# First pair of a seven-product down projection: another product order, other places for its weight sums, and two small moves on VectorE

## The chip, the cores and the metric

The kernel runs on one core of a Trainium2 chip. Its time is the device time of one execution in microseconds (us), taken as the median of several runs. Five engines work beside each other, each in the order of its own program: PE (TensorE) multiplies, DVE (VectorE) and ACT (ScalarE) work elementwise, POOL (GpSimd) works elementwise too, and SP (SyncE) issues the loads from HBM. Semaphores are the only link between them.

## What is computed

The reference is two transformer-like blocks on 512 tokens (528 in the first block, with 16 meta tokens), width 1024. Each block has two feed-forward layers (FFNs) around a mixer; the four FFNs are the same computation with different weights:

```python
def swiglu(x, w_in, w_out):
    gu = x @ w_in
    return (jax.nn.silu(gu[..., :D_FF]) * gu[..., D_FF:]) @ w_out
...
h = h + 0.5 * rmsnorm(swiglu(rmsnorm(h, gn[0]), ffn_w_in[i, 0], ffn_w_out[i, 0]), gn[1])
```

`D_FF` is 2816. The change lies in the last product, `@ w_out`, 2816 by 1024, of each of the four FFNs (numbered 0 to 3 here). Everything is float32.

## The kernel before

**Splitting.** PE multiplies in a reduced float32 format, so each operand is split into a high part (a copy, mostly on ACT: `hi`) and a low part (operand minus high part, on DVE or POOL: `lo`), and a product is three matmuls: high by high, high by low, low by high. Weight blocks of 128x1024 lie in four slots each of `raw` (as loaded), `whi`, `wlo`, and `stage` (sums of blocks).

**The down projection.** Of the 22 row tiles of `w_out`, 6 are multiplied directly, one unit per output tile (8 units; ACT's `keep(j)` moves unit j's result to SBUF). The other 16 are multiplied pair by pair (`PAIRS` is 4; a pair is two output tiles of 128 columns) by a scheme of seven products M1 to M7 in place of eight. A pair's weights are four loaded blocks A11, A21, A12, A22 and four sums: S1 = A21 + A22, S2 = S1 - A11, S3 = A11 - A21, S4 = A12 - S2 (functions `s1` to `s4`, DVE). The hidden values have blocks B and sums T in the same way (`x_hi`, `x_lo`, `x_sum`), and they are made once, during the units and the first pair. Products use M1: A11, M2: A12, M3: S4, M4: A22, M5: S1, M6: S2, M7: S3; each is 8 row tiles by 3 matmuls, 24 matmuls of 256 columns (264 in FFN 0), line L3396.

**Orders.** Everything is ordered by hand: `PRODUCTS`, `D_HI`, `LO_DVE`, `LO_POOL` and `D_POSTS` must name the order in which PE, ACT, DVE and POOL go, because each entry becomes a semaphore count. DVE also adds each product's bank to the output (`post`, lines L2174 in FFN 0 and 1 and L2176 in FFN 2 and 3): k1 takes M1, u2 takes M6, k5 M5, c22 M7, k23 M3, c21 M4. Products share PSUM banks, so M6 waits for k1, M7 for u2, M3 for k5, and M4 for c22. S1 and S2 of the first three pairs are written to PSUM banks 6 and 7 (`sums`), one after the other, so S2 waits until S1's low part is done. A slot of `whi` and `wlo` is given by a product's place in the order (`nth`), and ACT may write it when the product four places earlier is done. A block of `raw` may be loaded for the next pair when its readers are done (`block_read`); SP issues A11, A21, A12, A22 in that order.

**Lines.** DVE: `s1` L2226, `s2` L2237, `s3` L2241, `s4` L2250 (L2253 in the last pair); `lo` of a sum in PSUM L2262, of a raw block L2266, of a staged sum L2268; `x_lo` L2205; `merge` (FFN 2 and 3 only) L2212; `gained` (FFN 3 only) L2289; low parts of the next stage's input L1863. ACT: `hi` L970, `x_hi` L955, `keep` L947. POOL: `lo` L638. In the first pair POOL makes the low parts of A11 and A12, and then waits for the low part of T4 before it goes on to the second pair's A11.

Of the kernel before, what the change touches and what calls it, by code (L numbers as in the profile page):

```python
# [127 lines left out]
def program(nc, dram, out, stop=99):  # L128
# [210 lines left out]
    DOWN_TAKES = dict(mult=24, w_hi=27, w_sum=16, w_lo_dve=28, w_lo_pool=13, kept=8, x_diff=14, x_hi=14)  # L339
# [601 lines left out]
    def act_down(act, i):  # L941
# [15 lines left out]
        def hi(d, block):  # L957
# [1232 lines left out]
    def dve_down(v, i):  # L2190
# [24 lines left out]
        def s1(d):  # L2215
            down_loaded(v, i, d, "A21")
            down_loaded(v, i, d, "A22")
            if d == 0:
# [37 lines left out]
        def lo(d, block):  # L2256
# [1903 lines left out]
```

## Time and profile before

| | us |
|---|---|
| median of 3 runs | 1949.59 |
| range of the runs | 1948.12 to 1954.43 |
| span of the profiled execution | 1948.1 |
| PE, matmul busy in that span | 1907.9 (98%) |
| DVE busy | 1400.1 (72%) |
| ACT busy | 1027.5 (53%) |
| POOL busy | 878.1 (45%) |

The page lists busy time per engine. A matmul's row lasts longer than the step to the next one (rows of 0.28 us start about 0.12 us apart), so PE reads as busy across a short stall, and its idle figure is smaller than the time lost. Lost time is therefore read here from the starts of matmuls. In a timeline row the columns are start, duration, engine, line, operation, output and inputs, shape, count, and in brackets the idle time before it with what ended it. The span and the median differ by 1.5 us.

### The profile page before, as it was taken

To read this page: it belongs to the slowest core of one execution; us is meant where nothing else is said; L and a number is where in the kernel's file an instruction comes from. 1 tells how busy PE (TensorE), PEld (TensorE's weight loads), DVE (VectorE), ACT (ScalarE), POOL (GpSimd) and SP (SyncE) were. 2 spreads that over 40 slices of the span, in tenths; PEclk is the share of its full clock that TensorE was granted. 3 is DMA by queue.
4 is the path that set the end of the run, shared out by engine and by line. 5 is a ranking of instruction groups with operands and counts; after the bars stand their busy time and mean duration, and the time that the engine had idled before them with its cause. 6 is when DMAs were issued, how large, how long until landed. Compare 5 with 4: busy or idle time off the path is not lost. (4 is left out here: it accounts for less than half of the span.)

```text
span 1948.1 us, 38305 instructions
## 1 busy us (share of the span) xinstructions
PE 1907.9 (98%) x13945; PEld 1751.9 (90%) x13945; DVE 1400.1 (72%) x1936; ACT 1027.5 (53%) x1695; POOL 878.1 (45%) x525
## 2 busy tenths in 40 slices
PE   8999999999999999999999999999999999999998
PEld 8999999997779899989989998897775778999898
DVE  5977687785455877676787768877756548776876
ACT  5566654535324566664466666445346445666543
POOL 3455453643325455553545555344441044555533
PEclk9999999999999999999999999999999999999999
DMA  6233333322412233333423334243311022333332
GB/s 178 66 103 101 97 88 102 105 58 65 111 52 71 82 108 108 105 101 87 120 65 109 108 108 116 80 117 104 81 44 55 2 86 77 108 107 105 101 87 87
DMA packets 344605, 178.05 MB, mean 91 GB/s; under 512 B 18715, under 2 KB 340118, under 8 KB 344494
## 3 DMA queue, kind: packets, MB, share of 16 engines
q1 hardware_dynamic: 342640, 175.46, 31.8%
q8 instruction: 74, 1.21, 0.2%
q10 hardware_dynamic: 1854, 1.07, 0.2%
q14 instruction: 37, 0.30, 0.1%
HBM read 174.42 MB, written 2.10 MB: 91 GB/s over the span
## 5 line engine op out<-in xcount | busy, mean ns | idle before, releaser
L3458 PE MATMUL ps<-xop,whi 128*128 128x256 f32 (+1 forms) x4032 | 722.8, 282 | 8.6 <-DVE sq L2005 5.9
L3458 PEld LDWEIGHTS ps<-xop,whi 128*128 128x128 f32 x4032 | 621.1, 189 | 10.8 <-DVE sq L2005 6.8
L3458 PE MATMUL ps<-xop,wlo 128*128 128x256 f32 (+1 forms) x2016 | 568.1, 282 | 0.0
L536 POOL TENSOR_TENSOR wlo<-raw,whi 128x1024 fp32r<-128x1024 f32 x94 | 233.9, 2497 | 371.0 <-ACT whi L702 360.8
L3458 PEld LDWEIGHTS ps<-xop,wlo 128*128 128x128 f32 x2016 | 379.7, 188 | 0.0
L597 POOL TENSOR_TENSOR wlo<-raw,whi 128x512 fp32r<-128x512 f32 x212 | 278.2, 1323 | 220.7 <-ACT whi L832 219.9
L3396 PE MATMUL ps<-xop,whi 128*128 128x256 f32 (+1 forms) x896 | 215.1, 284 | 6.7 <-DVE hT L2176 1.8
L3129 PE MATMUL ps<-xhi,whi 128*128 128x512 f32 (+2 forms) x624 | 210.8, 367 | 1.7 <-DVE xlo L1863 1.6
L3129 PE MATMUL ps<-xlo,whi 128*128 128x512 f32 (+2 forms) x624 | 204.0, 356 | 0.0
L3129 PE MATMUL ps<-xhi,wlo 128*128 128x512 f32 (+2 forms) x624 | 203.5, 355 | 0.0
L3396 PE MATMUL ps<-hid_r,whi 128*128 128x256 f32 (+1 forms) x768 | 191.3, 283 | 2.9 <-DVE hT L2176 2.4
L638 POOL TENSOR_TENSOR wlo<-raw,whi 128x1024 fp32r<-128x1024 f32 x44 | 114.7, 2614 | 165.9 <-ACT whi L970 111.2
L597 POOL TENSOR_TENSOR wlo<-stage,whi 128x512 fp32r<-128x512 f32 x72 | 94.2, 1309 | 179.8 <-ACT whi L832 179.8
L3396 PEld LDWEIGHTS ps<-xop,whi 128*128 128x128 f32 x896 | 155.4, 188 | 9.8 <-DVE hT L2176 2.2
L832 ACT ACTIVATE whi<-ps 128x512 fp32r<-128x512 f32 x180 | 107.9, 599 | 106.6 <-DVE ps L1974 79.9
L3396 PE MATMUL ps<-xop,wlo 128*128 128x256 f32 (+1 forms) x576 | 162.2, 282 | 0.0
L1994 DVE TENSOR_TENSOR wlo<-ps,whi 128x512 fp32r<-128x512 f32 x180 | 123.4, 685 | 47.9 <-ACT whi L832 47.6
L3396 PEld LDWEIGHTS ps<-hid_r,whi 128*128 128x128 f32 x768 | 135.7, 188 | 5.1 <-DVE hT L2176 4.0
L832 ACT ACTIVATE whi<-raw 128x512 fp32r<-128x512 f32 x216 | 134.2, 621 | 0.0
L3129 PEld LDWEIGHTS ps<-xhi,whi 128*128 128x128 f32 (+1 forms) x624 | 109.5, 187 | 27.0 <-issue 6.0
L702 ACT ACTIVATE whi<-raw 128x1024 fp32r<-128x1024 f32 x96 | 99.8, 1051 | 63.2 <-PE ps L3129 49.0
L3129 PEld LDWEIGHTS ps<-xlo,whi 128*128 128x128 f32 (+1 forms) x624 | 110.0, 187 | 18.3 <-issue 2.2
(469 smaller groups left out, 3950.9 us busy)
## 6 DMA issues: line engine op xcount, KB each, us to landing
raw<-in_ffn_w_in SPq DMA_DIRECT2D x88, 512.0 KB, 3.8
raw<-in_ffn_w_gate SPq DMA_DIRECT2D x44, 512.0 KB, 3.8
raw<-in_ffn_w_up SPq DMA_DIRECT2D x44, 512.0 KB, 3.8
raw<-in_ffn_w_out SPq DMA_DIRECT2D x32, 512.0 KB, 4.2
raw<-in_ffn_w_down SPq DMA_DIRECT2D x32, 512.0 KB, 4.2
raw<-in_a_w_in SPq DMA_DIRECT2D x24, 512.0 KB, 3.9
raw<-in_w_in SPq DMA_DIRECT2D x19, 512.0 KB, 3.9
raw<-in_ffn_w_out SPq DMA_DIRECT2D x16, 384.0 KB, 3.5
```

The lines of the kernel that those rows point to most:

```text
L536: pool.tensor_tensor(wlo[:, u % SLOTS, :], raw[:, u % SLOTS, :], whi[:, u % SLOTS, :].bitcast(F32), ALU.subtract).then_inc(lo_done, 1)
L597: pool.tensor_tensor(operand(wlo, i, name), source, operand(whi, i, name).bitcast(F32), ALU.subtract) \
L638: ins = pool.tensor_tensor(to, source, down_operand(whi, i, d, block).bitcast(F32), ALU.subtract)
L702: act.activation(whi[:, s, :], raw[:, s, :], ACT.Copy).then_inc(hi_done, 1)
L832: ins = act.activation(operand(whi, i, name), source, ACT.Copy)
L1994: v.tensor_tensor(operand(wlo, i, name), sum_place(i, name), operand(whi, i, name).bitcast(F32), ALU.subtract).then_inc(s["w_lo_dve"], 1)
L3129: ins = pe.matmul(o, lhs[l], x[r], start=first and n == 0, stop=last and n == 2)
L3396: ins = pe.matmul(ps[:, bank_, 0:h], weights[l][:, k * P:(k + 1) * P], parts[r][:, k % 4, :], start=start and k == 0 and q == 0, stop=k == ...
L3458: ins = pe.matmul(to, w[l][:, k * P:(k + 1) * P], x[r][:, k * h:(k + 1) * h], start=start and k == 0 and q == 0, stop=k == 3 and q == 2, s ...
```

## The change

In pair 0, PE's order becomes M1, M2, M6, M5, M7, M3, M4 (M2 and M5 change places), and ACT's high parts follow it (A12 first, S1 last of its three). S2 gets PSUM banks of its own, 4 and 5, so it no longer waits for S1's low part. S3 is written over A21 in `raw`, so it needs no free slot of `stage` and is made right behind S2, ahead of k1; in return the next load into that place waits for S3's low part. In FFN 2 and 3, `merge(2)` and `merge(3)` move: one ahead of `s1`, one ahead of the two low parts. Behind k1 on DVE, k5 moves from second place to behind S4's low part, A22's low part moves ahead of B22's second low part, and the low part of pair 1's A11 is added, which POOL made before; POOL's wait for T4 goes. In pairs 1, 2 and 3, u2 moves ahead of a low part, and `gained` behind S4's low part.

```diff
-    DOWN_TAKES = dict(mult=24, w_hi=27, w_sum=16, w_lo_dve=28, w_lo_pool=13, kept=8, x_diff=14, x_hi=14)
+    DOWN_TAKES = dict(mult=24, w_hi=27, w_sum=16, w_lo_dve=29, w_lo_pool=12, kept=8, x_diff=14, x_hi=14)
...
-            sp.wait_ge(*down_sum(i, d, "S3"))
+            sp.wait_ge(*(down_lo(i, d, "S3") if d == 0 else down_sum(i, d, "S3")))
...
         for d in (1, 2):
-            if d == 1:
-                pool.wait_ge(*x_lo_made(i, "T4", 1))
-            lo(d, "A11")
+            if d == 2:
+                lo(d, "A11")
             lo(d, "A12")
...
-        hi(0, "S1")
+        hi(0, "A12")
         keep(6)
         hi(0, "S2")
         keep(7)
-        hi(0, "A12")
+        hi(0, "S1")
...
-    PRODUCTS = [["M1", "M5", "M6", "M2", "M7", "M3", "M4"]] * 3 + [["M1", "M2", "M6", "M4", "M7", "M5", "M3"]]
+    PRODUCTS = [["M1", "M2", "M6", "M5", "M7", "M3", "M4"]] + [["M1", "M5", "M6", "M2", "M7", "M3", "M4"]] * 2 + [["M1", "M2", "M6", "M4", "M7", "M5", "M3"]]
...
+    def sum_bank(d, block):
+        return ps[:, 4:6, :] if (block, d) == ("S2", 0) else ps[:, 6:8, :]
+
+    def s3_place(i, d):
+        return down_raw(i, d, "A21") if d == 0 else down_operand(stage, i, d, "S3")
...
+            elif d == 1:
+                v.wait_ge(*down_sum(i, 0, "S2"))
+                v.wait_ge(*down_lo(i, 0, "S1"))
...
-            if d < PAIRS - 1:
+            if d == 0:
+                v.wait_ge(*x_lo_made(i, "T2", 1))
+                v.wait_ge(*x_sum_made(i, "T4", 1))
+                to = sum_bank(d, "S2")
+            elif d < PAIRS - 1:
...
         def s3(d):
-            down_slot_free(v, i, d, "S3")
-            v.tensor_tensor(down_operand(stage, i, d, "S3"), down_raw(i, d, "A11"), down_raw(i, d, "A21"), ALU.subtract) \
+            if d == 0:
+                v.wait_ge(*down_sum(i, d, "S1"))
+            else:
+                down_slot_free(v, i, d, "S3")
+            v.tensor_tensor(s3_place(i, d), down_raw(i, d, "A11"), down_raw(i, d, "A21"), ALU.subtract) \
...
         merge(1)
+        merge(2)
         s1(0)
+        s2(0)
+        s3(0)
+        merge(3)
+        lo(0, "S2")
         lo(0, "S1")
-        s2(0)
-        lo(0, "S2")
-        merge(2)
-        merge(3)
         a, b, c = down_banks(0)
         post(0, "k1", "M1", 0, 0, a)
-        s3(0)
         x_lo("T3", 0)
-        post(0, "k5", "M5", 1, 1, c)
         x_lo("T3", 1)
         lo(0, "S3")
         s4(0)
+        x_lo("B22", 0)
         post(0, "u2", "M6", 0, 1, a)
-        x_lo("B22", 0)
+        lo(0, "A22")
         x_lo("B22", 1)
         lo(0, "S4")
-        lo(0, "A22")
+        post(0, "k5", "M5", 1, 1, c)
+        x_lo("T4", 0)
         post(0, "c22", "M7", 1, 1, a, "k5")
-        x_lo("T4", 0)
+        lo(1, "A11")
         x_lo("T4", 1)
         s1(1)
...
             s4(d)
+            post(d, "u2", "M6", 0, 1, a)
+            lo(d, "S4")
             gained(d - 1)
-            lo(d, "S4")
-            post(d, "u2", "M6", 0, 1, a)
...
+        post(3, "u2", "M6", 0, 1, a)
         lo(3, "S1")
-        post(3, "u2", "M6", 0, 1, a)
...
+            multiply(d, *(("M2", b) if d == 0 else ("M5", c)), True).then_inc(s["mult"], 1)
+            pe.wait_ge(*down_post(i, d, "k1"))
+            multiply(d, "M6", a, False).then_inc(s["mult"], 1)
             if d == 0:
                 pe.wait_ge(s["kept"], down_at[i]["kept"] + KD)
-            multiply(d, "M5", c, True).then_inc(s["mult"], 1)
-            pe.wait_ge(*down_post(i, d, "k1"))
-            multiply(d, "M6", a, False).then_inc(s["mult"], 1)
-            multiply(d, "M2", b, True).then_inc(s["mult"], 1)
+            multiply(d, *(("M5", c) if d == 0 else ("M2", b)), True).then_inc(s["mult"], 1)
```

The other lines of the diff carry the same orders into `LO_DVE`, `LO_POOL`, `D_HI` and `D_POSTS`, and the new places into `hi`, `s4` and `lo`.

## Rows read from the trace of the kernel before

**Rows 1.** The page: its first line and section 1 (busy us, share).

```profile
span 1948.1 us, 38305 instructions
PE 1907.9 (98%) x13945; PEld 1751.9 (90%) x13945; DVE 1400.1 (72%) x1936; ACT 1027.5 (53%) x1695; POOL 878.1 (45%) x525
```

**Rows 2.** PE's waits, whole run: us in total, times, longest us.

```profile
PE ps L3396 <- DVE hT L2176: 4.2, 7, 1.0
...
PE ps L3396 <- DVE ybuf L2174: 2.0, 3, 0.9
```

**Rows 3.** PE's timeline: pair 0's M1 and pair 3's M5, each FFN.

```profile
287.35 0.29 PE L3396 MATMUL ps<-xop,whi 128*128 128x264 f32 x1
...
290.27 0.29 PE L3396 MATMUL ps<-xop,whi 128*128 128x264 f32 x1
...
366.19 0.28 PE L3396 MATMUL ps<-xop,whi 128*128 128x264 f32 x1
...
878.54 0.28 PE L3396 MATMUL ps<-xop,whi 128*128 128x256 f32 x1
...
955.27 0.28 PE L3396 MATMUL ps<-xop,whi 128*128 128x256 f32 x1
...
1228.36 0.28 PE L3396 MATMUL ps<-xop,whi 128*128 128x256 f32 x1
...
1307.00 0.28 PE L3396 MATMUL ps<-xop,whi 128*128 128x256 f32 x1
...
1852.06 0.28 PE L3396 MATMUL ps<-xop,whi 128*128 128x256 f32 x1
...
1931.01 0.28 PE L3396 MATMUL ps<-xop,whi 128*128 128x256 f32 x1
```

**Rows 4.** PE's timeline, FFN 1: pair 1's M6, pair 3's M1, M2.

```profile
906.14 0.38 PE L3396 MATMUL ps<-xop,whi 128*128 128x256 f32 x1 [0.92 <-DVE ybuf L2174]
...
941.10 0.28 PE L3396 MATMUL ps<-xop,whi 128*128 128x256 f32 x1
...
943.94 0.28 PE L3396 MATMUL ps<-hid_r,whi 128*128 128x256 f32 x1
```

**Rows 5.** DVE's timeline, FFN 1, pair 0 and S1 of pair 1.

```profile
881.57 0.42 DVE L2174 TENSOR_TENSOR ybuf<-ybuf,ps 128x256 f32<-128x256 f32 x1 [4.25 <-PE ps L3396]
881.91 1.95 DVE L2241 TENSOR_TENSOR stage<-raw 128x1024 f32<-128x1024 f32 x1
883.78 1.21 DVE L2205 TENSOR_TENSOR xop<-xop_f,hid_r 128x1024 fp32r<-128x1024 f32 x1
884.92 0.41 DVE L2174 TENSOR_TENSOR ybuf<-ybuf,ps 128x256 f32<-128x256 f32 x1
...
892.39 1.21 DVE L2266 TENSOR_TENSOR wlo<-raw,whi 128x1024 fp32r<-128x1024 f32 x1
...
897.65 2.11 DVE L2226 TENSOR_TENSOR ps<-raw 128x1024 f32<-128x1024 f32 x1 [1.45 <-issue]
```

**Rows 6.** ACT's timeline, FFN 1, pair 0.

```profile
878.74 0.60 ACT L947 ACTIVATE ybuf<-ps 128x512 f32<-128x512 f32 x1 [2.68 <-PE ps L3129]
...
884.86 1.99 ACT L955 ACTIVATE xop<-hid_f 128x1024 fp32r<-128x1024 f32 x2
```

**Rows 7.** POOL's timeline, FFN 1, and the last row FFN 3.

```profile
880.36 2.42 POOL L638 TENSOR_TENSOR wlo<-raw,whi 128x1024 fp32r<-128x1024 f32 x1 [10.19 <-ACT whi L970]
896.28 2.39 POOL L638 TENSOR_TENSOR wlo<-raw,whi 128x1024 fp32r<-128x1024 f32 x1 [13.50 <-DVE wab_r L2205]
...
1925.13 2.71 POOL L638 TENSOR_TENSOR wlo<-stage,whi 128x1024 fp32r<-128x1024 f32 x1 [2.32 <-ACT whi L970]
```

**Rows 8.** DVE's timeline, FFN 2 (two rows) and FFN 3.

```profile
1229.01 2.35 DVE L2212 SCALAR_TENSOR_TENSOR hT<-ybuf,hT 128x1024 f32<-128x1024 f32 x2
...
1305.38 6.69 DVE L1863 SCALAR_TENSOR_TENSOR xlo<-hT,vec,xhi 128x512 fp32r<-128x512 f32 x4
...
1883.72 2.29 DVE L2289 TENSOR_SCALAR ybuf<-hT,vec 128x512 f32<-128x512 f32 x2
```

More of the change, by code:

```diff
@@ L963, in hi @@
             if block == "S1" or (block == "S2" and d < PAIRS - 1):
-                source, to = ps[:, 6:8, :], down_operand(whi, i, d, block).rearrange("p (a n) -> p a n", a=2)
+                source, to = sum_bank(d, block), down_operand(whi, i, d, block).rearrange("p (a n) -> p a n", a=2)
+            elif block == "S3":
+                source, to = s3_place(i, d), down_operand(whi, i, d, block)
             elif block == "S4" and d == PAIRS - 1:
@@ L1581, in program @@
     D_SUMS = [["S1", "S2", "S3", "S4"]] * 3 + [["S1", "S2", "S4", "S3"]]
-    D_HI = [["A11", "S1", "S2", "A12", "S3", "S4", "A22"]] + [["A11", "S1", "A12", "S2", "S3", "S4", "A22"]] * 2 \
+    D_HI = [["A11", "A12", "S2", "S1", "S3", "S4", "A22"]] + [["A11", "S1", "A12", "S2", "S3", "S4", "A22"]] * 2 \
         + [["A11", "A12", "S2", "A22", "S3", "S1", "S4"]]
-    LO_DVE = [(x, p) for x in ("T1", "B11", "T2", "B21") for p in range(2)] + [("S1", 0), ("S2", 0)]
-    LO_DVE += [("T3", 0), ("T3", 1), ("S3", 0), ("B22", 0), ("B22", 1), ("S4", 0), ("A22", 0), ("T4", 0), ("T4", 1)]
+    LO_DVE = [(x, p) for x in ("T1", "B11", "T2", "B21") for p in range(2)] + [("S2", 0), ("S1", 0)]
+    LO_DVE += [("T3", 0), ("T3", 1), ("S3", 0), ("B22", 0), ("A22", 0), ("B22", 1), ("S4", 0), ("T4", 0), ("A11", 1), ("T4", 1)]
     LO_DVE += [("S1", 1), ("S2", 1), ("S4", 1), ("S1", 2), ("S2", 2), ("S4", 2), ("S2", 3), ("S1", 3), ("S4", 3)]
-    LO_POOL = [("A11", 0), ("A12", 0)] + [(block, d) for d in (1, 2) for block in ("A11", "A12", "S3", "A22")]
+    LO_POOL = [("A11", 0), ("A12", 0)] + [(block, 1) for block in ("A12", "S3", "A22")]
+    LO_POOL += [(block, 2) for block in ("A11", "A12", "S3", "A22")]
     LO_POOL += [(block, 3) for block in ("A11", "A12", "A22", "S3")]
-    D_POSTS = [["k1", "k5", "u2", "c22", "k23", "c21"]] * 3 + [["k1", "k2", "u2", "k4", "c21", "c22", "k5", "u4", "c12"]]
+    D_POSTS = [["k1", "u2", "k5", "c22", "k23", "c21"]] + [["k1", "k5", "u2", "c22", "k23", "c21"]] * 2 + [["k1", "k2", "u2", "k4", "c21", "c22", "k5", "u4", "c12"]]
     ACC_AT = [1, 3, 5]
@@ L2249, in s4 @@
                 down_slot_free(v, i, d, "S4")
-                ins = v.tensor_tensor(wide(down_operand(stage, i, d, "S4")), wide(a12), sums, ALU.subtract)
+                ins = v.tensor_tensor(wide(down_operand(stage, i, d, "S4")), wide(a12), sum_bank(d, "S2"), ALU.subtract)
             else:
@@ L2261, in lo @@
             if block == "S1" or (block == "S2" and d < PAIRS - 1):
-                ins = v.tensor_tensor(wide(to), sums, wide(hi), ALU.subtract)
+                ins = v.tensor_tensor(wide(to), sum_bank(d, block), wide(hi), ALU.subtract)
+            elif block == "S3":
+                ins = v.tensor_tensor(to, s3_place(i, d), hi, ALU.subtract)
             elif block == "S4" and d == PAIRS - 1:
```

## The prediction

> **What bounds the kernel now.** I read the page first, then the list of what PE waited for, then PE's timeline in the four down projections, then DVE's, ACT's and POOL's timelines beside it. PE is busy for 98% of the span [rows 1], so the kernel is bound by PE and by the few places where PE stalls. At L3396, the seven-product part, it waited for DVE's posts for 6.2 us in ten waits [rows 2]. The list understates them: matmul rows of 0.28 us start 0.12 us apart, so a stall reads 0.16 us short, and a stalled product also starts with one slow step of about 0.1 us.
>
> The clean measure is from starts. An undisturbed product takes 943.94 - 941.10 = 2.84 us [rows 4], and 290.27 - 287.35 = 2.92 us in FFN 0, with its 264 columns [rows 3]. From M1 of pair 0 to M5 of pair 3 there are 26 products. FFN 0: 366.19 - 287.35 = 78.84, less 26 x 2.92 = 75.92, leaves 2.92 us lost. FFN 1: 955.27 - 878.54 = 76.73, less 26 x 2.84 = 73.84, leaves 2.89. FFN 2: 1307.00 - 1228.36 = 78.64 leaves 4.80. FFN 3: 1931.01 - 1852.06 = 78.95 leaves 5.11 [rows 3]. All four together lose 15.7 us; this is the most that the change can win here.
>
> The worst single stall is M6 of pair 1 [rows 4]: it waits for DVE's k1, which is queued behind the low part of S2. Behind it lies one chain. DVE sits idle for 4.25 us ahead of k1 in pair 0 and then works without a pause [rows 5]: S3, lows of T3, S4, lows of B22, S4 and A22, lows of T4. The load for pair 1's A22 is issued behind A22's low part (892.39 + 1.21 = 893.60), and S1 of pair 1 starts at 897.65, 4.05 us later [rows 5]. Then it takes 2.11 us in place of 1.21 because POOL's op of 896.28 to 898.67 lies across it [rows 5, 7]. PE reaches pair 1 before its operands do.
>
> **The change part by part**, for FFN 1. Steps on DVE, start to start: a 128x1024 op 1.14 us (883.78 to 884.92), a post 0.34 us (881.57 to 881.91) [rows 5]. On ACT a pair of 128x1024 ops takes 1.99, so 0.95 each [rows 6].
>
> *Ahead of k1.* S2, S3 and both low parts now lie there, one op more than before, in 4.25 us of idleness. S1's high part is last on ACT: `keep(7)` ends at 879.34 [rows 6], the high part at 880.3, the low part on DVE at 881.6. M1 ends and k1 starts at 881.57 [rows 5], so k1 starts as before, at most 0.1 later. S1 is now needed by the fourth product, at 887.1, not the second. S3's removal from behind k1 takes 1.95 us out of the busy chain [rows 5]. Cost: nothing while the idleness lasts.
>
> *Behind k1*, from 881.9: two lows of T3, low of S3, S4 and a low of B22 are 5 x 1.14, to 887.6; u2 (M6 ended by 887.2) to 887.9. A22's high part stands behind S4's on ACT: S4 is done at 886.5, two high parts later it is 888.6, so DVE waits 0.7 there. A22's low part ends at 889.8, 3.8 earlier than 893.60. Then low of B22, low of S4 and k5: k5 runs 892.0 to 892.4. M3, the sixth product, is due at 878.54 + 5 x 2.84 = 892.74; 0.3 to spare. That spare is the tightest point of the new order. Low of T4 to 893.5, c22 to 893.8, the added low part of pair 1's A11 to 895.0, low of T4 to 896.1. The load issued at 889.9 lands at about 893.9, so S1 of pair 1 no longer waits for it: it runs 896.1 to 897.3, undisturbed by POOL, and ends 2.4 us earlier than 899.76.
>
> *Pair 1 on PE*, due at 898.42, 901.26, 904.10 and so on. M1 needs A11's low part: 895.0, free. M5 needs S1's: high 898.4, low 899.6, free. M6 needs S2's and k1: S2 899.7 to 900.9, c21, high 901.9, low 903.2, k1 903.5; 0.5 to spare. M7 needs u2, which no longer waits for S4's high and low parts. So all of FFN 1's 2.89 us goes. The later pairs follow, since their loads and high parts are released by the same products earlier. FFN 0 goes the same way with 2.92 us (its chain has 0.5 to spare at M3).
>
> *FFN 2 and 3* have two merges of 1.14 each ahead of k1 [rows 8], and the second waits for `keep(7)` and stands ahead of both low parts. `keep(7)` ends 0.8 us after M1's start (879.34 to 878.54 in FFN 1), and with 3 x 1.14 behind it k1 begins at 4.2 and ends at 4.7, where it ended at 3.4; M6 is due at 5.7, free. The rest of the chain is as long as above, so k5 ends about 1.0 after M3 is due, and 1.1 us of stall stays with the slow step. FFN 2 keeps 1.1 of 4.80, a gain of 3.7 at M5 of pair 3. But its end is bound by DVE: four low parts for the mixer (6.69 us, stretched by POOL) stand between k4 and c21 [rows 8]; they follow M4's end, which comes 3.0 earlier, and less if POOL falls differently. I take 2.8, between 2.5 and 3.7. FFN 3 keeps 1.1 as well. POOL's low part of S3 in pair 3 ends at 1927.84 [rows 7], 0.3 before M7 begins there (1931.01 - 2.84 = 1928.17), and should move up somewhat less than PE; I leave 0.36 for it, an estimate between 0 and 0.7: 5.11 - 1.1 - 0.36 = 3.65.
>
> *Bounds of what no row shows.* S2 and S4 at other PSUM banks, and S3 written in place, are the same shapes as before; I price them at nothing, between -0.1 and +0.5 per FFN (a slip beyond the 0.3 spare). A21's next load now waits for S3's low part, at 885.4; it is issued ahead of A22's, which is issued at 889.9, so it costs nothing until it slips 4.5 us. The load could only win time by being bound by nothing else. POOL loses one op of 2.4 us; it is mostly idle there [rows 7].
>
> *Sum.* 2.92 + 2.89 + 2.8 + 3.65 = 12.3 us, off the profiled span of 1948.1: 1935.8. The median stands 1.5 above that span, so 1949.59 - 12.3 = 1937.3. What follows each stage (squares, norms, the next weights) starts from the last products' ends, so I let the gain pass through.
>
> A rule weighed here: S1's stretch to 2.11 us under POOL's op shows that the two engines exclude each other [rows 5, 7]. The Trainium skill, page "SBUF — State Buffer", section "SBUF: two separate sides", says that VectorE and GpSimd share a pair of ports as an exclusive lock, held for a whole instruction, also against a VectorE op with a fast mode; the trace agrees with the stretch. By that rule `gained` is at risk in its new place, the fifth rival below.
>
> **The rivals.**
> 1. *k5 becomes the wait.* DVE is the busier party in pair 0, with 0.3 us to spare. One op held by POOL (0.9 as in S1's row) on that chain would cost 0.4 + 0.6 + 0.9 + 0.9 = 2.8 us: 1940.1. A hold of a whole POOL op, 2.4 less what overlaps, about 2.1: 7.6 us, 1944.9. Against it: POOL has nothing to do between the low parts of A12 in pair 0 and in pair 1.
> 2. *The end takes it back.* If pair 3's chains of DVE, POOL and ACT do not move up with PE, FFN 2 wins nothing and the others half: (2.92 + 2.89 + 3.65) / 2 = 4.7 gained, 1944.9. Against it: their releasers are products and posts of pairs 2 and 3.
> 3. *Everything goes*, the 1.1 us in FFN 2 and 3 too: 1949.59 - 15.7 = 1933.9. For it: the 0.7 wait for A22's high part could shrink.
> 4. *Slower.* POOL's wait for T4's low part kept it off DVE for 13.50 us [rows 7]. Without it, POOL could start pair 1's A12 inside the chain from k1 to S1. Each hit costs DVE up to 2.4. It decides when two hits fall into each FFN: 4 x 2 x 2.4 = 19.2 less 12.3 gained is +6.9, 1956.5. Against it: ACT's high part of A12 stands behind that of S1 of pair 1, which comes after the chain.
> 5. *`gained` held.* In FFN 3 the two scalings (2.29 us, of which the first is stretched) [rows 8] now follow S4's low part, so two POOL ops in a row can hold them, and c22 stands behind them. I find c22 ends 0.2 to 0.4 before M4 needs it; one more hold of 1.1 in pairs 1 and 2 costs about 1.6: 1938.9.
>
> **How the numbers follow.** Forecast, 12.3 us less: 0.64, own range 1935.5 to 1939.5. Rival 1: 0.15, half of it below 1943.7. Rival 2: 0.07. Rival 3: 0.06. Rival 4: 0.04. Rival 5: 0.04. A measurement of this kernel can tell about 0.3% from no change, 5.85 us, so faster begins at 1943.7: 0.64 + 0.08 + 0.06 + 0.04 + 0.02 of rival 2, where it takes back less, = 0.84. Slower: 0.04. The rest, 0.12, is within 0.3%. The range reaches from rival 3 to the cheaper half of rival 1: 1934.0 to 1943.5.
>
> **What would show it.** In the profile after: M1 of pair 0 to M5 of pair 3 takes 75.9 in FFN 0, 73.8 in FFN 1, about 74.9 in FFN 2 and 75.3 in FFN 3; M6 of pair 1 has no idle time; S1 of pair 1 starts right behind T4's low part and lasts 1.2; M3 of pair 0 stalls in FFN 2 and 3 alone, for k5. A stall at M3 of pair 0 in FFN 0 and 1, or an S1 of pair 1 that still waits for its load, would make the prediction wrong.

## The result, and the profile after

The changed kernel takes 1942.4 us (median of 11 runs, 1937.13 to 1947.7) and the kernel before, on the same chips, 1949.75 us (11 runs, 1948.12 to 1960.35). The estimated ratio is 0.995, 95% interval 0.9935 to 0.9965: 9.7 us faster, between 6.8 and 12.7. The medians themselves lie 7.35 us apart, and the profiled executions 7.5 us (1948.1 to 1940.6). The forecast was 1937.3, 12.3 us faster.

The page of the changed kernel, its first line and section 1; beside them stand [rows 1]:

```profile
span 1940.6 us, 38305 instructions
PE 1901.8 (98%) x13945; PEld 1749.8 (90%) x13945; DVE 1414.5 (73%) x1940; ACT 1026.6 (53%) x1695; POOL 866.7 (45%) x521
```

Four ops (one in each FFN) went from POOL to DVE, as the diff says. PE's waits in the whole run, in us in total, times, longest; `multiply` is now L3417, and the waits of [rows 2] read:

```profile
PE ps L3180 <- DVE sqbuf L1891: 5.9, 3, 4.9
...
PE ps L3417 <- DVE hT L2184: 2.0, 2, 1.0
...
PE ps L3417 <- POOL wlo L638: 0.9, 2, 0.5
```

The 6.2 us of waits for DVE's posts in the seven-product part have become 2.0. But a line that was small before is now among the longest: 5.9 us at L3180, 4.9 of them in one wait. In the kernel before, the same line (L3159) had 1.6 us in all.

PE's timeline, M1 of pair 0 and M5 of pair 3 in each FFN, as in [rows 3]:

```profile
287.28 0.29 PE L3417 MATMUL ps<-xop,whi 128*128 128x264 f32 x1
...
363.42 0.28 PE L3417 MATMUL ps<-xop,whi 128*128 128x264 f32 x1
...
881.17 0.28 PE L3417 MATMUL ps<-xop,whi 128*128 128x256 f32 x1
...
955.10 0.28 PE L3417 MATMUL ps<-xop,whi 128*128 128x256 f32 x1
...
1227.52 0.28 PE L3417 MATMUL ps<-xop,whi 128*128 128x256 f32 x1
...
1303.06 0.28 PE L3417 MATMUL ps<-xop,whi 128*128 128x256 f32 x1
...
1847.75 0.28 PE L3417 MATMUL ps<-xop,whi 128*128 128x256 f32 x1
...
1923.43 0.28 PE L3417 MATMUL ps<-xop,whi 128*128 128x256 f32 x1
```

| M1(0) to M5(3), us | before | forecast | after | gain |
|---|---|---|---|---|
| FFN 0 | 78.84 | 75.9 | 76.14 | 2.70 |
| FFN 1 | 76.73 | 73.8 | 73.93 | 2.80 |
| FFN 2 | 78.64 | 74.9 | 75.54 | 3.10 |
| FFN 3 | 78.95 | 75.3 | 75.68 | 3.27 |

Of the 15.7 us that these stretches lost before, 11.9 are gone. So the part that was changed does what was forecast. The place where the time went can be read from the starts: M1 of FFN 1 begins at 881.17, where it began at 878.54 before. FFN 0 ended 2.77 us earlier (363.42 against 366.19), and FFN 1 starts 2.63 us later. Between them lies the first block's mixer, which the change does not touch.

The timeline of the changed kernel there (ACT, POOL, DVE and PE, in the order of the argument), and then stretches of 5 us (first their length, then the busy time of PE, PEld, DVE, ACT and POOL; the granted clock is third from the end):

```profile
392.81 2.00 ACT L701 ACTIVATE whi<-raw 128x1024 fp32r<-128x1024 f32 x2
393.93 5.12 POOL L536 TENSOR_TENSOR wlo<-raw,whi 128x1024 fp32r<-128x1024 f32 x2 [3.50 <-ACT whi L701]
390.65 6.21 DVE L1881 TENSOR_TENSOR sqbuf<-sqbuf 128x528 f32<-128x528 f32 x6
396.89 2.73 DVE L1891 TENSOR_TENSOR sqbuf<-sqbuf 128x528 f32<-128x528 f32 x1
399.67 2.29 PE L3180 MATMUL ps<-ones,sqbuf 128*128 128x1 f32 x10 [4.93 <-DVE sqbuf L1891]
```

```profile
395.00:400.00 5.00, 0.33 (x2) 0.33 (x2) 4.58 (x2) 0.00 (x0) 4.05 (x2) 0.90 0.23 13
400.00:405.00 5.00, 5.00 (x24) 4.72 (x23) 0.85 (x5) 0.27 (x1) 0.00 (x0) 0.50 0.39 108
405.00:410.00 5.00, 5.00 (x40) 5.00 (x40) 3.11 (x5) 1.96 (x3) 0.00 (x0) 0.92 0.07 16
```

DVE adds up the squares of eight tiles; PE's column sums wait for the last add. POOL's two low parts, released by ACT, begin at 393.93 in the middle of the adds, and the adds are held while POOL's ops run: the last takes 2.73 us in place of 0.71. This is called the collision below. PE idles 4.93 us, and then works for more than 5 us at a granted clock of 0.50, the lower level of 1.2 GHz. The same rows of the kernel before:

```profile
396.90 2.00 ACT L702 ACTIVATE whi<-raw 128x1024 fp32r<-128x1024 f32 x2
398.03 5.29 POOL L536 TENSOR_TENSOR wlo<-raw,whi 128x1024 fp32r<-128x1024 f32 x2 [4.83 <-ACT whi L702]
393.41 4.03 DVE L1873 TENSOR_TENSOR sqbuf<-sqbuf 128x528 f32<-128x528 f32 x6
397.48 0.71 DVE L1883 TENSOR_TENSOR sqbuf<-sqbuf 128x528 f32<-128x528 f32 x1
398.68 1.17 PE L3159 MATMUL ps<-ones,sqbuf 128*128 128x1 f32 x10
```

```profile
375.00:380.00 5.00, 4.72 (x36) 4.54 (x36) 5.00 (x8) 2.28 (x7) 4.83 (x4) 0.92 0.05 11
380.00:385.00 5.00, 5.00 (x34) 5.00 (x33) 4.53 (x12) 3.36 (x7) 2.55 (x4) 0.74 0.32 94
```

There POOL began at 398.03, when the last add was all but done. Between the same two matmuls on either side of the column sums (384.7 to 403.3 before, 380.6 to 407.2 after) the mixer took 18.6 us and takes 26.6, 8.0 us more. One thing in the comparison matters for the cause. DVE's adds moved up by 393.41 - 390.65 = 2.76 us, as far as FFN 0's end (2.77); ACT's op moved by 396.90 - 392.81 = 4.09. The difference of 1.3 us is the stretch at 375 to 385 of the kernel before, in which PE ran at 1.2 GHz (0.92 and 0.74 granted) and which the profiled execution after does not have. PE, and with it ACT, whose op stands behind one that waits for PE, and POOL behind ACT, got ahead of DVE by that.

So the account of the two profiled executions is: 11.9 us gained in the four changed stretches, 1.3 more because the clock held at 375 to 385, 8.0 lost between the two matmuls in the mixer, and 2.3 gained in small pieces in the stages between (1.3 from the mixer to FFN 1, 0.7 from FFN 1's end to FFN 2, 0.4 from FFN 2's end to FFN 3): 7.5. The small pieces are no effect of the change that can be told from noise: two executions of the changed kernel differ in the first two of these stages by 1.0 and 1.5 us.

### The profile page after: what moved, and what is told of

Its sections match the earlier page's. It is cut to its first block and busy times, and to the rows that moved or that the text cites. A ratio compares the mean times of both kernels' runs of the same rounds, so it can differ in the third digit from the quotient of the medians.

```text
span 1940.6 us, 38305 instructions
## 1 busy us (share of the span) xinstructions
PE 1901.8 (98%) x13945; PEld 1749.8 (90%) x13945; DVE 1414.5 (73%) x1940; ACT 1026.6 (53%) x1695; POOL 866.7 (45%) x521
## 3 DMA queue, kind: packets, MB, share of 16 engines
q10 hardware_dynamic: 1854, 1.07, 0.2%
## 5 line engine op out<-in xcount | busy, mean ns | idle before, releaser
L536 POOL TENSOR_TENSOR wlo<-raw,whi 128x1024 fp32r<-128x1024 f32 x94 | 234.0, 2498 | 376.9 <-ACT whi L701 366.7
L3417 PE MATMUL ps<-xop,whi 128*128 128x256 f32 (+1 forms) x896 | 213.9, 283 | 2.0 <-DVE hT L2184 2.0
L3417 PE MATMUL ps<-hid_r,whi 128*128 128x256 f32 (+1 forms) x768 | 190.1, 282 | 0.9 <-POOL wlo L638 0.9
L638 POOL TENSOR_TENSOR wlo<-raw,whi 128x1024 fp32r<-128x1024 f32 x40 | 103.5, 2596 | 167.4 <-ACT whi L971 167.2
L3417 PE MATMUL ps<-xop,wlo 128*128 128x256 f32 (+1 forms) x576 | 162.3, 282 | 0.0
L3417 PEld LDWEIGHTS ps<-xop,whi 128*128 128x128 f32 x896 | 155.6, 189 | 2.8 <-DVE hT L2184 2.4
L3417 PEld LDWEIGHTS ps<-hid_r,whi 128*128 128x128 f32 x768 | 135.9, 188 | 1.6 <-issue 1.4
```

The costliest lines, as they stand in the source:

```text
L536: pool.tensor_tensor(wlo[:, u % SLOTS, :], raw[:, u % SLOTS, :], whi[:, u % SLOTS, :].bitcast(F32), ALU.subtract).then_inc(lo_done, 1)
L638: ins = pool.tensor_tensor(to, source, down_operand(whi, i, d, block).bitcast(F32), ALU.subtract)
L3417: ins = pe.matmul(ps[:, bank_, 0:h], weights[l][:, k * P:(k + 1) * P], parts[r][:, k % 4, :], start=start and k == 0 and q == 0, stop=k == ...
```

## Experiments

For each kernel "lost" is the time from pair 0's M1 to pair 3's M5 beyond 26 undisturbed products, as in the forecast, read from PE's starts and summed over the four FFNs. Between the executions whose seven-product part has the same code (before and b_guard; after, a_again and a_guard) its sum repeats to 0.4 us, while the whole times of one kernel spread over 2 to 12 us, so verdicts on parts rest on it. A wait of one product, below, is the idle figure of its row and the 0.16 us by which that reads short.

| kernel | us, median (range), runs | lost, us (FFN 0, 1, 2, 3) |
|---|---|---|
| before | 1949.75 (1948.12 to 1960.35), 11 | 15.7 (2.92, 2.89, 4.80, 5.11) |
| after | 1942.4 (1937.13 to 1947.7), 11 | 3.9 (0.22, 0.10, 1.70, 1.84) |
| a_again | 1940.35 (1938.33 to 1947.7), 6 | 3.8 (0.23, 0.06, 1.69, 1.85) |
| a_guard | 1937.87 (1937.15 to 1939.67), 6 | 4.2 (0.22, 0.38, 1.74, 1.86) |
| b_guard | 1951.52 (1947.5 to 1955.29), 12 | 15.9 (2.98, 2.64, 4.70, 5.53) |
| bg_u2 | 1947.57 (1946.84 to 1949.69), 10 | 12.9 (2.65, 2.46, 3.72, 4.02) |
| ag_no_u2 | 1939.18 (1938.08 to 1944.82), 4 | 7.1 (0.56, 0.56, 2.55, 3.45) |
| ag_lo11_pool | 1938.53 (1936.84 to 1941.18), 4 | 4.0 (0.45, 0.04, 1.37, 2.18) |
| ag_a22_late | 1938.47 (1935.83 to 1938.88), 4 | 3.0 (-0.08, -0.17, 1.71, 1.54) |
| ag_k5_late | 1944.7, 1 | 8.5 (1.41, 0.84, 3.68, 2.60) |
| ag_merge3 | 1935.86 (1934.01 to 1937.2), 4 | 1.5 (0.24, 0.24, 0.36, 0.66) |
| ag_merge3_sq | 1938.66 (1936.04 to 1938.8), 5 | 1.6 (0.22, 0.21, 0.48, 0.73) |
| ag_merge3b | 1937.76 (1937.1 to 1940.58), 5 | 3.1 (0.25, -0.06, 1.31, 1.60) |
| ag_merge3b_sq_u2 | 1936.06 (1934.83 to 1936.75), 5 | 1.9 (0.24, -0.18, 0.74, 1.09) |

### Is it the collision? a_again, a_guard, b_guard

Expected of the changed kernel for a second time:

> The changed kernel itself, unchanged, for a second profile of it. Theory A: the 5 us that are missing were lost in the first mixer, where PE, now 2.8 us earlier, lets ACT and so POOL start a low part while DVE still adds up squares; POOL's 2.5 us ops hold those adds, PE idles 4.9 us and then runs at 1.2 GHz for about 5 us. Whether it happens hangs on where PE stands by a microsecond or two, so by A this profile either shows PE idle again for 3 to 5 us ahead of the column sums of the first mixer (1940 to 1946 us) or shows less than 1.5 us of idleness there (1935 to 1939 us). Rival B: the time is lost in no fixed place, the spread of 1937 to 1948 us is noise of the whole execution; then the time is no function of that idleness. Both: the four down projections take the same time as before to 0.2 us (76.1, 73.9, 75.5 and 75.7 us from pair 0's M1 to pair 3's M5).

Its profiled execution had the same collision: PE idle for 4.9 us ahead of the column sums, DVE's adds 6.21 and 2.73 us long, and 26.7 us between the two matmuls named above. Its span was 1945.9 us. The four stretches took 76.15, 73.90, 75.53 and 75.69 us, so what varies from run to run is not there. The two executions share the collision and still differ by 5.3 us, so the collision isn't all of the spread.

One line is added for a_guard to the changed kernel, and for b_guard to the kernel before:

```diff
         pool_transition(pool, 0, u, U_M1)
+        pool.wait_ge(norm_s["summed"], norm_at[1]["summed"] + 1)
```

> The changed kernel with one wait more: behind the first mixer's additions POOL waits until DVE has added up the squares, then goes on with its low parts. Theory A: DVE's adds take 4.7 us in place of 8.9, PE's idleness ahead of the column sums falls from 4.9 us to under 1.2, the clock stays at 2.4 GHz there, and the time is 1935.5 us, between 1933.5 and 1938, with less spread from run to run than the 10 us of the changed kernel. Rival B (the collision is no cause): 1942 us as before, spread as before. A third case, that POOL's later start starves PE of low parts: PE waits for POOL at the next products and the time is 1938 to 1942 us.

> The kernel before with the same wait of POOL. In its profiled execution there was no collision (POOL began 0.2 us before DVE's last add ended), since PE had lost 1.4 us at 1.2 GHz just ahead of it. Theory A: about 1948 us, between 1946.5 and 1949.5; what it can gain is only in executions in which the collision falls. Then the changed kernel with the wait is 11 to 13 us faster than this one: the forecast's 12.3 us. Rival B: 1949.6 us, and the distance to the changed kernel with the wait stays 7 to 9 us.

The timeline of a_guard (DVE, POOL, PE), and two stretches:

```profile
391.18 4.04 DVE L1882 TENSOR_TENSOR sqbuf<-sqbuf 128x528 f32<-128x528 f32 x6
395.25 0.71 DVE L1892 TENSOR_TENSOR sqbuf<-sqbuf 128x528 f32<-128x528 f32 x1
396.20 4.88 POOL L536 TENSOR_TENSOR wlo<-raw,whi 128x1024 fp32r<-128x1024 f32 x2 [5.24 <-DVE sqbuf L1892]
396.43 1.17 PE L3181 MATMUL ps<-ones,sqbuf 128*128 128x1 f32 x10
```

```profile
375.00:380.00 5.00, 5.00 (x32) 5.00 (x32) 4.56 (x9) 2.67 (x6) 4.72 (x5) 0.67 0.38 105
395.00:400.00 5.00, 5.00 (x42) 4.83 (x43) 1.78 (x7) 1.97 (x4) 3.80 (x2) 1.00 0.06 6
```

The adds take 4.04 and 0.71 us as in the kernel before, PE does not idle ahead of the column sums, the clock stays at 1.00 behind them, and the stretch between the two matmuls is 18.6 us. But this one execution doesn't test the collision: its clock fell at 376.7 (0.67 granted from 375 to 380), as in the kernel before, and ACT's high part, from 394.65 on, was so late that POOL waited only some 0.4 us for the adds. The test is an execution with the wait in which the clock held. ag_merge3 below has one, and up to this point its program is that of a_guard (ACT, POOL, DVE, PE):

```profile
392.93 2.00 ACT L702 ACTIVATE whi<-raw 128x1024 fp32r<-128x1024 f32 x2
395.79 4.76 POOL L536 TENSOR_TENSOR wlo<-raw,whi 128x1024 fp32r<-128x1024 f32 x2 [5.22 <-DVE sqbuf L1893]
390.78 4.03 DVE L1883 TENSOR_TENSOR sqbuf<-sqbuf 128x528 f32<-128x528 f32 x6
395.61 1.28 PE L3183 MATMUL ps<-ones,sqbuf 128*128 128x1 f32 x10 [0.73 <-DVE sqbuf L1893]
```

ACT begins 2.15 us behind the first add, as in the changed kernel (2.16), but POOL now starts only when the adds are done. They take 4.03 and 0.71 us, PE idles 0.73 us in place of 4.93, and the stretch between the two matmuls is 19.6 us in place of 26.6. Three more kernels with the wait in which the clock held there (ag_lo11_pool, ag_merge3b_sq_u2, and ag_no_u2, where it fell only sooner) have 19.6 as well. So the collision costs 7.0 us at the same clock; the other 1.0 of the 8.0 is PE, which comes to the column sums 1.3 us sooner and waits for adds that don't.

The median of a_guard is 1937.87 us with a spread of 2.5 us, where the changed kernel had 10.6, and 9.4 the second time. Against the kernel before on the same chip (1949.87) that is 12.0 us, ratio 0.9921 (0.9902 to 0.9941). The changed kernel without the wait took 1940.35 there, ratio 0.9933 (0.9912 to 0.9953): on whole times alone the two intervals overlap, and what carries the case is the stage. The profiled executions of a_guard and of the kernel before had the same fall of the clock and the same 37.13 us from M5 of FFN 0 to the second of the two matmuls; they lie 11.6 us apart, 11.5 of them in the four stretches. So without the collision the gain passes through, and the forecast of 1937.3 was the time of the change without it. Some expectations missed: I gave 1935.5 as the likeliest, and the third case, POOL's late start, shows in a_guard only as a wait of 0.2 us that the kernel before has too (0.4 to 0.8 us, near 444, in the kernels in which the clock held).

b_guard is not faster than the kernel before (ratio 0.9995, 0.9981 to 1.0009). So the wait alone brings nothing that can be told from noise, which fits a collision that is rare or absent there; its profiled execution, which had none, lost time in other stretches at 1.2 GHz (370 to 390 and 970 to 980 us). Its median lies above the 1946.5 to 1949.5 us that I expected, and 13.7 us above that of a_guard, where I expected 11 to 13. One part of theory A falls: I had put the collision down to PE's being 2.8 us earlier. DVE's adds were earlier by as much. What differs is the 1.3 us for which the clock did or did not fall some 13 us behind M5 of FFN 0 (379.2 in the kernel before). All 14 profiled executions agree with that: in the eight with this dip ACT's op begins 3.4 to 4.5 us behind the first add, and in the six without it 2.2; DVE's seven undisturbed adds take 4.8. The kernels without the wait follow: before, with the dip, no collision; after and a_again, without it, a collision each. (In a_again the clock fell sooner, 3 us behind M5, which made DVE late too and left the distance at 2.2.) What decides on that dip no run shows. The three profiled kernels with the old order of pair 0 have it, and five of the eleven with the new order; that is too few to say that the change makes it rarer, so whether the change itself brings the collision stays open.

### Which part won what? bg_u2, ag_no_u2, ag_lo11_pool, ag_a22_late

From here on every kernel has the wait of POOL. The two small moves alone, on the kernel before:

```diff
             s4(d)
+            post(d, "u2", "M6", 0, 1, a)
+            lo(d, "S4")
             gained(d - 1)
-            lo(d, "S4")
-            post(d, "u2", "M6", 0, 1, a)
...
+        post(3, "u2", "M6", 0, 1, a)
         lo(3, "S1")
-        post(3, "u2", "M6", 0, 1, a)
```

> The kernel before with the wait of POOL in the first mixer (as b_guard), and of the change only the two small moves in pairs 1 to 3: u2 ahead of a low part, gained behind S4's low part. Theory A (the two parts of the change take away different stalls): the stalls at M7 of pairs 1 and 2 go, those of pair 0, and M1, M5 and M6 of pair 1, stay. From pair 0's M1 to pair 3's M5: FFN 0 0.2 to 0.3 us less than the kernel before, FFN 1 0.5 less, FFN 2 1.0 less, FFN 3 2.6 less (gained stood ahead of u2 there), 4.5 in all, so 4.5 us under b_guard. Rival (the stalls at M7 are late followers of the late start of pair 1): they stay, and nothing changes.

And the changed kernel with this diff undone:

> The changed kernel with the wait of POOL (as a_guard), but u2 and gained of pairs 1 to 3 at their old places. Theory A: M7 of pairs 1 and 2 stalls again, 0.3 us in FFN 1, 0.8 in FFN 2, 2.4 in FFN 3, and nothing in FFN 0: 3.5 us over a_guard, about 1941.4 us. Rival (with pair 1 started in time the u2 places are hidden): 1937.9 us as a_guard.

bg_u2 lost 12.9 us where b_guard lost 15.9: 3.0 us, less than the 4.5 expected. All waits of M7 in pairs 1 and 2 are gone (1.10 and 1.09 us in FFN 3 of b_guard), and those of M3 in pair 0 and of M1, M5 and M6 in pair 1 stay at their sizes; but in FFN 1 M7 of pair 3 now waits 0.3 us, and in FFN 3 0.6, for POOL's low part of S3. ag_no_u2 lost 2.9 us more than a_guard (3.5 expected). M7 waits again, in FFN 3 0.99 and 1.07 us. Its DVE timeline in FFN 3, pair 1, shows why:

```profile
1878.13 2.28 DVE L2310 TENSOR_SCALAR ybuf<-hT,vec 128x512 f32<-128x512 f32 x2
1880.33 1.21 DVE L2289 TENSOR_TENSOR wlo<-stage,whi 128x1024 fp32r<-128x1024 f32 x1
1881.47 0.41 DVE L2185 SCALAR_TENSOR_TENSOR hT<-ps,hT 128x256 f32<-128x256 f32 x1
```

u2 (the last row) stands behind `gained` and S4's low part and ends at 1881.88; M7 starts at 1881.93. So the parts add up: the small moves are worth 2.9 to 3.0 us with or without the rest, and the new order of pair 0 with its sums 15.85 - 7.12 = 8.7 us.

The added low part back on POOL:

```diff
         for d in (1, 2):
-            if d == 2:
-                lo(d, "A11")
+            if d == 1:
+                pool.wait_ge(*x_lo_made(i, "T4", 1))
+            lo(d, "A11")
...
-        lo(1, "A11")
```

> The changed kernel with the wait of POOL (as a_guard), but the low part of pair 1's A11 back on POOL, behind its wait for T4's low part. On DVE this frees 1.14 us ahead of S1 of pair 1, but POOL's 2.4 us op lies across S1 again. Theory A (POOL's op holds S1): S1 of pair 1 starts about 1.1 us sooner than in a_guard, lasts 2 us or more in place of 1.2, ends at most 0.3 us sooner, and the products of pair 1 are as in a_guard: the time is within 1 us of a_guard. Rival (the low part moved to DVE is what saved pair 1): M1 of pair 1 stalls 0.3 us or more in each FFN and M6 of pair 1 up to 1 us, 2 to 5 us over a_guard.

Lost: 4.0 us, a_guard 4.2. The move from POOL to DVE is worth nothing that can be seen in the sum. In it, M1 of pair 1 loses 0.7 us over the four FFNs, and M7 of pair 3 waits about 1 us less than in a_guard, so the move does take a small wait away. Where I was wrong is the hold. The timeline in FFN 1, S1 of pair 1 on DVE, A11's low part on POOL, and M1 of pair 1 on PE:

```profile
893.34 1.22 DVE L2239 TENSOR_TENSOR ps<-raw 128x1024 f32<-128x1024 f32 x1
893.50 3.31 POOL L638 TENSOR_TENSOR wlo<-raw,whi 128x1024 fp32r<-128x1024 f32 x1 [20.75 <-DVE wab_r L2215]
896.86 0.38 PE L3418 MATMUL ps<-xop,whi 128*128 128x256 f32 x1
```

S1 starts 1.14 us sooner, as expected, but lasts 1.22 us: it began 0.16 us ahead of POOL's op, and this time POOL's op is the one that stretches, to 3.31 us in place of 2.4. Before, S1 had been late for its load, started inside POOL's op and waited for it [rows 5, 7]. M1 of pair 1 then waits 0.10 to 0.24 us for the low part.

A22's low part behind k5:

```diff
         post(0, "u2", "M6", 0, 1, a)
-        lo(0, "A22")
         x_lo("B22", 1)
         lo(0, "S4")
         post(0, "k5", "M5", 1, 1, c)
+        lo(0, "A22")
```

> The changed kernel with the wait of POOL (as a_guard), but the low part of pair 0's A22 behind k5, near its old place, where the next A22 is released later. Theory A (two ends meet here: k5 for M3, and the load of A22 for S1 of pair 1): DVE no longer waits 0.6 us for A22's high part, k5 runs 1.2 us sooner or more, M3 of pair 0 stalls nowhere (it stalled 1.1 us in FFN 2 and 3, 0.2 in FFN 0); the load lands 2.4 us later, so that S1 of pair 1 waits for it and starts about 0.4 us later than in a_guard, and M6 of pair 1 stalls 0 to 0.3 us. In all 1 to 2.4 us under a_guard. Rival (the release of A22 is the tighter end): S1 of pair 1 starts 1 us or more later, M6 of pair 1 stalls 0.5 to 1 us in all four, and the time is at or above that of a_guard.

M3 of pair 0 waits nowhere, and 1.2 us are won in all (lost 3.0), at the lower end of the expectation. In FFN 0 and 1 S1 of pair 1 starts 0.5 us sooner, not later, since DVE no longer waits for A22's high part. In FFN 2 and 3 the other end shows. DVE (S1 of pair 1, k1) and PE (M6 of pair 1) in FFN 2:

```profile
1243.04 1.23 DVE L2238 TENSOR_TENSOR ps<-raw 128x1024 f32<-128x1024 f32 x1 [0.64 <-issue]
1250.19 0.41 DVE L2185 SCALAR_TENSOR_TENSOR hT<-ps,hT 128x256 f32<-128x256 f32 x1
1250.66 0.39 PE L3418 MATMUL ps<-xop,whi 128*128 128x256 f32 x1 [0.85 <-DVE hT L2185]
```

S1 waits 0.64 us, as I read it for the load of A22 (the profile names no releaser; the block's low part ended at 1238.66, 4.4 us before), and M6 of pair 1 then waits 1.0 us for k1. S1 starts as late as in a_guard; PE, which no longer waits at M3, is 1.1 us sooner. The early place of A22's low part thus matters, but only by less than k5's place does, and only where M3 no longer hides it.

### How tight was k5? ag_k5_late

```diff
-        post(0, "k5", "M5", 1, 1, c)
         x_lo("T4", 0)
+        post(0, "k5", "M5", 1, 1, c)
```

> The changed kernel with the wait of POOL (as a_guard), with k5 one op later on DVE, behind the first low part of T4: the price of a k5 that is 1.14 us late. Theory A (k5 is the tightest point of the new order, with 0.2 to 0.3 us to spare in FFN 1 and none in the others): M3 of pair 0 waits 1.3 us in FFN 0, 0.9 in FFN 1, 2.3 in FFN 2 and 3, that is 4.3 us more than a_guard in all, about 1942 us. Rival (the low part of S4 is what M3 waits for, and k5 has an op's time to spare): no more than 1 us in all.

M3 waits 1.37, 0.92, 2.24 and 2.23 us, 6.8 in all against 2.4 in a_guard, as expected. (The lost time is also 4.3 us more, 8.5 against 4.2, but by chance: M7 of pair 3 waits 1.35 us less, and FFN 2 had a stretch at 1.2 GHz that cost about as much.) One op of 1.14 us ahead of k5 costs nearly its full length at M3 in every FFN: k5 is the tightest point of the new order.

### What is left: ag_merge3, ag_merge3_sq, ag_merge3b, ag_merge3b_sq_u2

The last merge behind `gained` in pair 1 (the counts of posts follow it):

```diff
-        merge(3)
         lo(0, "S2")
         lo(0, "S1")
...
             gained(d - 1)
+            if d == 1:
+                merge(3)
             post(d, "c22", "M7", 1, 1, a, "k5")
```

> The changed kernel with the wait of POOL (as a_guard), and the last merge taken out of the way of k1: it goes behind gained in pair 1. Theory A (in FFN 2 and 3 the two merges ahead of k1 make k5 late for M3): k1 and all behind it on DVE run 1.14 us sooner in FFN 2 and 3, M3 of pair 0 waits 0 to 0.2 us there in place of 1.1, S1 of pair 1 starts 1.1 us sooner or as soon as its load allows, and the moved op fits into DVE's idleness in pair 1. 2.2 us under a_guard, about 1935.7 us. Rival (A22's high part on ACT, and not the merges, sets k5): DVE waits 1.7 us for A22's high part in place of 0.6, k5 is as late as before, and the time stays at 1937.9 us.

M3 no longer waits in FFN 2 and 3, and 1.5 us are lost in place of 4.2. The time is 1935.86 us, ratio 0.9925 (0.991 to 0.9941) to the kernel before. In FFN 3 M4 of pair 1 now waits 0.66 us for c22, behind the moved op. M7 of pair 3 still waits for POOL's low part of S3. For that, ACT's squares ahead of A22's high part:

```diff
-        hi(3, "A22")
         square(2)
+        hi(3, "A22")
```

> As ag_merge3, and in pair 3 ACT's squares change places with A22's high part, so that POOL's low part of A22 starts behind S3's start on DVE. Theory A (POOL's op over S3 makes S3 last 3.1 us in place of 1.2 and so POOL's low part of S3, and M7 of pair 3, late): S3 lasts 1.2 us, M7 of pair 3 no longer waits 0.5 to 0.6 us in FFN 1, 2 and 3, 1.4 us under ag_merge3, about 1934.3 us, and nearly all that the seven-product parts lost is gone. Rival (POOL's op now falls on DVE's squares and u2 behind it, or A22's low part comes late for M4): M4 or M7 of pair 3 waits 0.5 us or more, and the time is that of ag_merge3 or above it.

FFN 2, pair 3, in ag_merge3 (POOL's low part of A22, DVE's S3):

```profile
1286.54 2.93 POOL L638 TENSOR_TENSOR wlo<-raw,whi 128x1024 fp32r<-128x1024 f32 x1 [4.93 <-ACT whi L972]
1287.45 3.10 DVE L2261 TENSOR_TENSOR stage<-raw 128x1024 f32<-128x1024 f32 x1
```

and in ag_merge3_sq (POOL; then S3, the sums of squares and u2 on DVE; then M7 on PE):

```profile
1289.31 2.75 POOL L638 TENSOR_TENSOR wlo<-raw,whi 128x1024 fp32r<-128x1024 f32 x1 [6.59 <-ACT whi L972]
1292.02 2.86 POOL L638 TENSOR_TENSOR wlo<-stage,whi 128x1024 fp32r<-128x1024 f32 x1
1288.58 1.22 DVE L2261 TENSOR_TENSOR stage<-raw 128x1024 f32<-128x1024 f32 x1
1290.14 2.48 DVE L2303 TENSOR_TENSOR acc<-acc,sq 128x512 f32<-128x512 f32 x1
1292.65 2.78 DVE L2305 TENSOR_TENSOR acc<-acc,sq 128x512 f32<-128x512 f32 x1
1295.36 0.41 DVE L2186 SCALAR_TENSOR_TENSOR hT<-ps,hT 128x256 f32<-128x256 f32 x1
1295.82 0.39 PE L3420 MATMUL ps<-hid_r,whi 128*128 128x256 f32 x1 [0.38 <-DVE hT L2186]
```

The rival holds. S3 takes 1.22 us, but POOL's two ops now lie over the two sums of squares (0.7 us each otherwise), u2 stands behind them, and M7 waits 0.54 us for u2 in place of 0.45 for the low part. The hold was moved, not removed, and nothing is won.

Two more places were tried: the last merge behind c22 in pair 2, and with it the exchange on ACT and, on DVE, u2 and S1's low part ahead of the sums of squares (each a move of one or two lines).

> As ag_merge3, but the last merge goes behind c22 in pair 2, where DVE waits 3.3 us for a load. Theory A (in ag_merge3 the moved op stood ahead of c22 in pair 1 of FFN 3, next to gained, and so M4 of pair 1 waited 0.66 us there): that wait is gone, M3 of pair 0 waits nowhere but 0.2 us in FFN 0, M7 of pair 3 waits 0.3 to 0.6 us in FFN 1, 2 and 3; lost in the four seven-product parts together 1.3 to 2.0 us, the time 1935.5 us, 2 us or more under a_guard. Rival (DVE has no room in pair 2 either): a product of pair 3 waits for S3 or for k1, the time 1936.5 us or more.

> As ag_merge3b, with the exchange of squares and A22's high part on ACT (as ag_merge3_sq), and on DVE u2 and the low part of S1 ahead of the sums of squares in pair 3. Theory A (in ag_merge3_sq POOL held the sums of squares in place of S3, and u2 stood behind them): the sums of squares are still held, but nothing that PE needs stands behind them, M7 of pair 3 waits less than 0.1 us in FFN 1 and 2, all four parts together lose under 1 us, and the time is 0.7 to 1.2 us under ag_merge3b. Rival (the held ops come late for something behind pair 3: the low part of S4, the last squares, the low parts of the next stage): M3 of pair 3 or the stage after waits, and nothing is won or some is lost.

In ag_merge3b M4 of pair 1 waits no more, but M7 of pair 3 waits 1.24 us in FFN 2 and 3 for POOL's low part of S3: 3.1 lost, the rival. In ag_merge3b_sq_u2 M7 waits nowhere; M4 of pair 3 waits 0.55 us for A22's low part instead, and M6 of pair 3 0.2 to 0.4: 1.9 lost, 1936.06 us, ratio 0.9923 (0.991 to 0.9937). That is 1.2 us less lost than in ag_merge3b, the upper end of the gain expected, but not the loss of under 1 us, and no better than ag_merge3. By their medians these two are the fastest versions: some 14 us under the kernel before, where the change alone is 7 to 10.

## Why the prediction was right, and what it left out

- *Bound and loss* (15.7 us, in the places named): right. bg_u2 and ag_no_u2 show that these stalls go separately, by 3.0 and 8.7 us.
- *The chain behind k1*: right to a few hundredths. After the change FFN 1 begins 2.63 us later; with that, k1 was forecast to start at 884.20, k5 at 894.63 and S1 of pair 1 at 898.73. The timeline of DVE has:

```profile
884.21 0.42 DVE L2182 TENSOR_TENSOR ybuf<-ybuf,ps 128x256 f32<-128x256 f32 x1
...
891.24 1.23 DVE L2286 TENSOR_TENSOR wlo<-raw,whi 128x1024 fp32r<-128x1024 f32 x1 [0.61 <-ACT whi L971]
...
894.65 0.41 DVE L2182 TENSOR_TENSOR ybuf<-ybuf,ps 128x256 f32<-128x256 f32 x1
...
898.72 1.23 DVE L2237 TENSOR_TENSOR ps<-raw 128x1024 f32<-128x1024 f32 x1
```

  S1 lasts 1.23 us, and no product of pair 1 waits in any FFN. The wait for A22's high part is 0.61 us (0.7 forecast).
- *M3 in FFN 2 and 3*: 1.1 us each forecast, 1.13 and 1.14 measured. FFN 0 was said to have 0.5 us to spare there and loses 0.19: a term of 0.2 us, mis-sized, and strictly one of the two signs that I had named for being wrong.
- *FFN 2*: two terms were mis-sized, with opposite signs. "FFN 2 keeps 1.1 of 4.80" left out M7 of pair 3, which had waited 0.56 us for u2 and still waits 0.56, now for POOL's low part of S3, since POOL's op still lies over S3 (3.09 us in both kernels); so 3.1 was won at M5, not 3.7. But the end, from which I took off 0.9, took off nothing: FFN 3 begins 4.31 us earlier, where FFN 2 had begun 0.84 earlier, 3.5 in all.
- *FFN 3*: 3.65 forecast, 3.27 measured; M7 of pair 3 waits 0.63 us where I left 0.36.
- *The sum*: 12.3 forecast; the four stretches won 11.9, and the stages behind the last three of them gave or took nothing beyond what varies between executions. With the collision kept off, the changed kernel is 12.0 us faster.
- *The step that failed* is the one sentence "What follows each stage (squares, norms, the next weights) starts from the last products' ends, so I let the gain pass through." It put the stages behind at nothing without a look at who stands beside whom in them. FFN 0's gain did pass to the end of the stage, and DVE moved up by all of it. But in the mixer behind it POOL's low parts began just as DVE's adds ended (398.03 against 397.48 + 0.71 = 398.19), and 1.3 us of clock decided between 18.6 and 26.6 us. No rival was about a stage outside the change. The measured 1942.4 lies above the forecast's own 1935.5 to 1939.5; that it lies within the range of 1934.0 to 1943.5 is luck, due to the width I gave to rival 1, which did not happen: its mechanism would have shown at M3 of pair 0, not in the mixer.
- *Rivals.* k5 late: not so, but its price is now measured (1.14 us on DVE, four times, cost M3 4.3 us in all). The end takes it back: no. Everything goes: no, the 1.1 us stayed; ag_merge3 gets them. Slower, by POOL in the chain: POOL's first op of pair 1 in FFN 1 begins at 902.41, behind the chain. `gained` held: M4 of pair 2 in FFN 3 waits 0.03 us at most.
- *The rule weighed there.* Rows first: in ag_lo11_pool DVE's S1 started 0.16 us ahead of POOL's op and POOL's op took 3.31 us; in the collision POOL's ops were under way and DVE's add took 2.73 us in place of 0.71. The Trainium skill, page "SBUF — State Buffer", section "SBUF: two separate sides", says that between a POOL op that reads SBUF and a DVE op with two inputs in SBUF, whichever starts first has the shared pair of ports for its whole instruction. The traces agree: S1 and the adds are such ops. By it the mixer could have been listed as a rival: two engines on one pair of ports, with nothing to spare between them.

What stays open: in how many executions of the changed kernel the collision falls (both profiled ones had it; the runs without a profile can't be asked), and why the clock fell some 13 us behind M5 of FFN 0 in eight of the profiled executions and not in six.

## What to carry to other kernels

A shift of one or two microseconds between engines can decide which of POOL and DVE holds the other, in stages that the change does not touch: after summing the gains, walk through the stages behind, and list each place where a POOL op starts within a microsecond or two of a DVE op on SBUF that PE waits for. Here such a place was cured by a wait that keeps POOL off until the DVE chain is done, since POOL had the time to spare; exchanging the order of ops only moved the hold to the next ops behind (ag_merge3_sq). To see gains of a few microseconds through noise of the same size, measure the stage from matmul to matmul, which repeated to 0.4 us here, and not the whole run. And before a profiled execution is taken to show that a cure works, look whether the harm would have struck in it: in a_guard's, with the same fall of the clock as the kernel before, it most likely would not have.

## What was not expected of the hardware

- In the transitions behind FFN 0 and FFN 1 (365 to 390 and 960 to 980 us), just behind groups of one-column matmuls (sums over columns, 376.83 to 378.98 in the kernel before), PE's clock falls to 1.2 GHz for some 3 us, once for twice as long, in some executions and not in others. In 14 profiled executions the part from M5 of FFN 0 to the first of the two matmuls in the mixer took 17.2 us (four, the changed kernel's first among them), 18.5 to 18.8 (seven), 19.7 and 19.9, or 21.5: steps of 1.3 to 1.6 us, one for each such stretch (two for the long one). The code of these kernels is the same there but for POOL's wait.
- A lost microsecond can help: the stretch at 1.2 GHz in the kernel before cost 1.3 us, of which 0.3 were left behind the column sums (37.1 us from M5 to the second matmul, against 36.8 in the kernels with the wait whose clock held), and with it POOL's op came too late to hold DVE's adds, which the other two unguarded profiles paid with 7.0.
- The hold between DVE and POOL works in both directions: a POOL op that starts 0.16 us behind a DVE op takes 3.31 us in place of 2.4.
